# The next expert's rows: gathered in quarters and turned by VectorE, in a decoder trunk with experts

## The reference

```python
def moe_swiglu(h, router, w_gate, w_up, w_down):
    t = h.reshape(B * S, D)                                   # 256 x 1024
    top_vals, top_idx = lax.top_k((t @ router), TOP_K)        # TOP_K = 2
    gates = jax.nn.softmax(top_vals, axis=-1)
    combine = jnp.sum(jax.nn.one_hot(top_idx, N_EXPERTS) * gates[..., None], axis=1)
    out = jnp.zeros_like(t)
    for e in range(N_EXPERTS):                                # 8; w_gate[e], w_up[e] are 1024 x 3584, w_down[e] 3584 x 1024
        out = out + combine[:, e:e + 1] * swiglu(t, w_gate[e], w_up[e], w_down[e])
    return out
```

## Time and profile before

| | us |
|---|---|
| Median of three runs (lowest, highest) | 1290.2 (1289.7, 1292.92) |
| Profiled execution | 1289.74 |
| Its span, first to last instruction | 1287.9 |
| TensorE busy | 1272.9 (99%) |
| TensorE weight loads | 745.1 (58%) |
| VectorE busy | 383.6 (30%) |
| ScalarE busy | 246.4 (19%) |
| GpSimd busy | 62.5 (5%) |
| DMA, mean rate over the span | 333 GB/s |
| TensorE's granted clock, mean | 0.998 |

### The profile page before, as it was taken

The page is one execution under the profiler, slowest core; times in us unless marked ns, Lnnn a source line. Parts: engine busy times, 40 slices in busy tenths (PEclk is TensorE's granted clock), DMA queues, the critical chain, the costliest instruction groups (busy, mean ns, idle before and its releaser), DMA issues.

```text
span 1287.9 us, 30972 instructions
## 1 busy us (share of the span) xinstructions
PE 1272.9 (99%) x14108; PEld 745.1 (58%) x14108; DVE 383.6 (30%) x664; ACT 246.4 (19%) x367; POOL 62.5 (5%) x63
## 2 busy tenths in 40 slices
PE   9999999999999999999999999999999999999997
PEld 7888888888785455336335534633543453363354
DVE  6976766568753120111002012010201201110022
ACT  6774443454631100100010010001001001000102
POOL 3000000000100001000100100010010010001000
PEclk9999999999999999999999999999999999999999
DMA  9646653755259999999999999999999999999991
GB/s 316 224 144 198 206 184 122 231 192 163 74 205 395 407 412 427 412 392 421 409 403 413 416 413 396 424 409 400 417 410 408 406 424 412 397 417 409 406 375 45
DMA packets 105690, 429.29 MB, mean 333 GB/s; under 512 B 5990, under 2 KB 42576, under 8 KB 89184
## 3 DMA queue, kind: packets, MB, share of 16 engines
q1 hardware_dynamic: 100336, 417.70, 82.3%
q0 software_dynamic: 4816, 8.59, 2.6%
q10 hardware_dynamic: 416, 1.09, 0.2%
HBM read 421.05 MB, written 6.31 MB: 332 GB/s over the span
## 4 chain that ended last, share of the span: by engine, by line
PE 95%; issue 2%; DVE 2%; ACT 1%; POOL 0%; DVEq 0%; POOLq 0%; ACTq 0%
PE bank L1716 93%; PE bank L2211 1%; PE bank L1759 0%; PE bank L1956 0%; ACT h L1015 0%; ACT work L1015 0%; POOL split_area L853 0%; DVE x L1665 0%; DVE split_area L643 0%; DVE work L1511 0%; PE bank L2165 0%; DVE split_area L1264 0%; DVE h L1365 0%; ACT work L1026 0%; DVE work L1436 0%
## 5 line engine op out<-in xcount | busy, mean ns | idle before, releaser
L1716 PE MATMUL bank<-raw_area,late_area 128*32 128x448 f32 (+1 forms) x5760 | 438.6, 464 | 0.0
L1716 PE MATMUL bank<-late_area 128*32 128x448 f32 (+1 forms) x5760 | 438.4, 464 | 0.0
L1716 PEld LDWEIGHTS bank<-raw_area,late_area 128*32 128x32 f32 x5760 | 205.6, 110 | 223.3 <-issue 177.0
L1716 PE MATMUL bank<-split_area 128*128 128x512 f32 (+1 forms) x1848 | 331.0, 339 | 1.1 <-DVE split_area L1264 0.8
L1716 PEld LDWEIGHTS bank<-late_area 128*32 128x32 f32 x5760 | 194.3, 110 | 238.1 <-issue 180.9
L1716 PEld LDWEIGHTS bank<-split_area 128*128 128x128 f32 x1848 | 283.4, 189 | 42.6 <-issue 4.1
L643 DVE TENSOR_TENSOR split_area<-raw_area,split_area 128x2048 fp32r<-128x2048 f32 (+1 forms) x56 | 123.4, 2209 | 47.0 <-ACT split_area L621 47.0
L621 ACT CAST split_area<-raw_area 128x2048 fp32r<-128x2048 f32 (+1 forms) x59 | 107.7, 1833 | 71.7 <-PE bank L1716 70.0
L1627 DVE COPY slot_sum<-next_slots 32x3 f32<-32x3 f32 x96 | 15.2, 159 | 305.6 <-DMA sum_dram<-qT,slot_row 279.1
L1646 DVE SCALAR_TENSOR_TENSOR work<-bank,slot_sum,work 128x448 f32<-128x448 f32 x48 | 32.8, 684 | 233.0 <-PE bank L1716 229.4
L1141 ACT COPY late_area<-bank 128x384 f32<-128x384 f32 x9 | 4.3, 478 | 433.9 <-PE bank L2211 433.9
(11 more groups left out here) (207 smaller groups left out, 421.5 us busy)
## 6 DMA issues: line engine op xcount, KB each, us to landing
raw_area<-in_moe_w_gate SPq DMA_DIRECT2D x32, 1792.0 KB, 14.5
late_area<-in_moe_w_gate SPq DMA_DIRECT2D x32, 1792.0 KB, 13.6
raw_area<-in_moe_w_up SPq DMA_DIRECT2D x32, 1792.0 KB, 14.6
late_area<-in_moe_w_up SPq DMA_DIRECT2D x32, 1792.0 KB, 15.2
raw_area<-in_moe_w_down SPq DMA_DIRECT2D x32, 1536.0 KB, 13.0
late_area<-in_moe_w_down SPq DMA_DIRECT2D x32, 1536.0 KB, 12.4
raw_area<-in_sb_w_qkv SPq DMA_DIRECT2D x12, 1024.0 KB, 5.3
raw_area<-in_ffn_w_down SPq DMA_DIRECT2D x11, 1024.0 KB, 4.9
```

The lines of the kernel that those rows point to most:

```text
L1716: return nc.tensor.matmul(out, lhsT, rhs, start=start, stop=stop, **kw)
```

## The change

GpSimd gathers the next expert's rows in three transfers, one for each chunk of slots. The copy of `h` in DRAM is seen as four rows of 256 features for each token, and partition `32 q + s` of a chunk gets quarter `q` of slot `s`. VectorE's transpose turns blocks of 32 x 32 in place, so that partition `32 q + f` of tile `t` holds feature `256 q + 32 t + f`. It does so behind its last block of up; TensorE's transposes, the two copies out of PSUM and their banks' uses go. Since the features now lie in another order on partitions, a gate or up load takes, for tile `t`, four blocks of 32 rows of the matrix, 256 rows apart. The first gather, on TensorE, makes the same order with four products of 32 stationary columns where it had one of 128. The spreading of slots over partitions moves to behind "next", as the gathers' row numbers come from it. TensorE waits for the turned rows at the start of an item, and the last scatter waits for the banks of up in place of those of the gather.

```diff
@@ SyncE, expert_loads
-                        src = a["moe_w_" + kind][0][bass.ds(e, 1), t * P:(t + 1) * P, :].rearrange("o d f -> (o d) f")
-                        sp.dma_start(slot, src).then_inc(arrived, 16)
+                        src = a["moe_w_" + kind][0][bass.ds(e, 1), :, :].rearrange("o (q t f) n -> t (o q) f n", q=GROUPS, t=DT)
+                        sp.dma_start(slot, src[t]).then_inc(arrived, 16)
@@ GpSimd
             def rows_for_next(i):
-                taken(pool, "next", i)
-                pool.sem_inc(pool_steps, 1)
-                pool.indirect_dma_start(out=h_rows, out_offset=None, in_=h_dram[:, :],
-                                        in_offset=bass.IndirectOffsetOnAxis(next_token[0:CAP, 0:1], 0)).then_inc(rows_gathered, 16)
+                pool.wait_ge(next_rows_ready, i * CHUNKS + CHUNKS)
+                for c in range(CHUNKS):
+                    pool.sem_inc(pool_steps, 1)
+                    pool.indirect_dma_start(out=h_rows[:, c, :], out_offset=None, in_=h_dram[:, :],
+                                            in_offset=bass.IndirectOffsetOnAxis(next_row[c][:, 0:1], 0)).then_inc(rows_gathered, 16)
@@ ScalarE, item
-                gathered_part("gather", i)
@@ VectorE
+            def slots_spread():
+                steps.settle()
+                for j in range(GROUPS):
+                    for c in range(CHUNKS):
+                        ins = V.tensor_copy(next_sum[j * QUAD:(j + 1) * QUAD, c, :], next_slots[c * QUAD:(c + 1) * QUAD, :])
+                link(ins)
 
             def item(i):
                 dve.wait_ge(summed, i * SUMS + SUM_STARTS)
-                for j in range(GROUPS):
-                    for c in range(CHUNKS):
-                        ins = V.tensor_copy(slot_sum[j * QUAD:(j + 1) * QUAD, c, :], next_slots[c * QUAD:(c + 1) * QUAD, :])
-                link(ins)
+                link(V.tensor_copy(slot_sum[:, :, :], next_sum[:, :, :]))
...
                 p = full(dve, "next", i)
-                steps.mark(V.tensor_copy(next_slots[0:CAP, :], p[0:CAP, 0:3]))
-                freed(V.tensor_copy(next_token[0:CAP, :], p[0:CAP, 0:1]), "next")
+                freed(V.tensor_copy(next_slots[0:CAP, :], p[0:CAP, 0:3]), "next")
+                taken(dve, "next", i)
+                slots_spread()
+                for c in range(CHUNKS):
+                    V.scalar_tensor_tensor(next_row[c][:, :], next_sum[:, c, 0:1], float(GROUPS), quarter[:, c:c + 1],
+                                           ALU.mult, ALU.add).then_inc(next_rows_ready, 1)
...
-                gathered_part("gather", i)
+                dve.wait_ge(rows_gathered, i * (16 * CHUNKS) + 16 * CHUNKS)
+                for c in range(CHUNKS):
+                    V.transpose(gathered[:, :, c * QUAD:(c + 1) * QUAD],
+                                h_rows[:, c, :].rearrange("p (t f) -> p t f", t=DT)).then_inc(gathered_ready, 1)
@@ TensorE
             def first_gather():
-                for q in range(2):
-                    pe.wait_ge(h_ready, TB + 1 + q)
-                    b = begin(pe, ("first gather", q))
-                    for n in range(4):
-                        for tb in range(TB):
-                            t = 4 * q + n
-                            ins = mm(b[:, n * CAP:(n + 1) * CAP], h[:, tb, t * P:(t + 1) * P], place[:, tb, :],
-                                     tb == 0, tb == TB - 1)
-                    filled(ins, ("first gather", q))
-            def transposed_rows(i):
-                pe.wait_ge(rows_gathered, i * 16 + 16)
-                for q in range(2):
-                    b = begin(pe, ("gather", q), i)
-                    for n in range(4):
-                        t = 4 * q + n
-                        ins = nc.tensor.transpose(b[:, n * CAP:(n + 1) * CAP], h_rows[:, t * P:(t + 1) * P], ident[0:CAP, 0:CAP])
-                    filled(ins, ("gather", q))
+                outs = [begin(pe, ("first gather", part)) for part in range(2)]
+                for tb in range(TB):
+                    pe.wait_ge(h_ready, DH * (tb + 1))
+                    for part in range(2):
+                        for n in range(HALF_T):
+                            for q in range(GROUPS):
+                                c0 = q * OUT + (part * HALF_T + n) * QUAD
+                                ins = mm(outs[part][quad(q), n * CAP:(n + 1) * CAP], h[:, tb, c0:c0 + QUAD], place[:, tb, :],
+                                         tb == 0 and n == 0, tb == TB - 1, skip_group_check=True)
+                        if tb == TB - 1:
+                            filled(ins, ("first gather", part))
...
-                    if j == 1:
-                        transposed_rows(i)
...
-            def item(i):
-                begin(pe, ("g", 1), i)
+            def item(i, first=False):
+                if first:
+                    taken(pe, ("first gather", 0))
+                else:
+                    pe.wait_ge(gathered_ready, i * CHUNKS)
```

## The result

The changed kernel takes 2983.2 us, median of six runs (2972.8 to 3000.9), beside 1290.1 us (1289.7 to 1293.1) for the kernel before on the same chip: a ratio of 2.312, interval 2.3066 to 2.3175. The profiled execution took 2993.52 us for a span of 2991.8. Predicted were 2900 us, with 2780 to 3025 as the range of its own case (A), and 2780 to 5080 with that of rival B.

The account below looks back on a forecast made before the run. TensorE's matmuls bound the kernel before; afterwards four engines' loads would. Their work from 358.6 us ends at 2857, and tail and end give 2881 us at full clock or 2927 at the lower; taken 2900, range 2780 to 5080.

Parts of the forecast that it names:

- case (A): Gate and up loads: four engines, each at its present rate; 2780 to 3025 us, chance 0.50.
- rival B: Gate and up loads: four engines, pairs sharing one way into memory, 34.3 us a load; 3025 to 5080 us, chance 0.32.
- Four engines for a load: Gate and up loads: outermost dimension 4 leaves 4 engines where 16 served; 12 fewer small packets a load.
- 17.15 us a load: Gate and up loads: each of four engines moves 458,752 B at 26.75 GB/s, 17.15 us instead of 4.3.
- The sum: Four engines' work from 358.6 us: 2178 gate and up, 287 down, 33.5 software queue; last down landed at 2857 us.
- The tail: TensorE's work behind the last down landing: 9.9 us at full clock, 55.7 at 1.2 GHz.
- dropped transposes: TensorE's chain in each item: 0.81 us x 8 = 6.5 us off, lost if four engines serve the loads.
- The lag of the loads: Gate and up loads on sixteen engines: issue to landing grows to 23 us at the end, under 31.9, so not binding.
- rival C: Gate and up loads: all sixteen engines share them by rows, transposes' gain stays; 1282.8 us, chance 0.13.
- Rival D: Loads on sixteen engines, but scattered memory places or small gather packets cost the queue; 1287 to 1292 us, chance 0.05.

Follow-up runs that it names:

- old line: Changed kernel with each gate or up load again one block of 128 matrix rows, everything else of the change kept: 1285.23 us, ratio 0.9956.
- every-eighth kernel: Changed kernel with features ordered 8 p + t, so a load takes every eighth matrix row, 128 at one pitch: 1285.55 us, ratio 0.9958.

## Why the prediction was right, point by point

**Four engines for a load: right.** Small packets fall from 5990 to 4710, by 1280: twelve for each of 128 loads is 1536, less 256 small ones that three gathers in place of one add to the software queue (5072 packets for the 4816 of the earlier trace rows). On the queue of the loads itself the count is exact: 100336 packets before, 98800 after, 1536 fewer. The mean busy share of sixteen engines is 0.395, within the 0.3 to 0.5 named. Two and eight blocks follow the same cut. The Trainium skill, "DMA: Bandwidth & Descriptors", section "Why a DMA increments its semaphore by 16 and not by 1", had the rule, and the traces agree in all these counts.

**17.15 us a load: right**, 17.1 measured, and 34.2 and 8.55 beside it.

**Engines in each other's way, rival B: it happens, but not for long.** The trace of after shows the first gate load alone and the time behind it:

```profile
338.00:342.00 4.00, 3.78 (x24) 3.05 (x23) 2.42 (x4) 3.65 (x5) 0.83 (x1) 1.00 0.26 61
...
354.00:358.00 4.00, 4.00 (x22) 3.48 (x22) 3.34 (x4) 2.45 (x4) 0.39 (x1) 1.00 0.27 79
...
374.00:378.00 4.00, 4.00 (x20) 3.30 (x19) 1.39 (x1) 0.36 (x1) 0.00 (x0) 1.00 0.25 104
```

Four engines are busy throughout, yet they move 61 GB/s, then 79, then 104, and the first load is through after some 28 us (the rates of 334 to 362 us add up to its 1.8 MB); the 19 us of A and the 36 of B were both off. As the text put it, an engine that runs some rows ahead frees both; the rates with four and, later on, with eight blocks fit that. A loss that looks the same comes back behind down, for some 40 us in the item shown and for less in others. The runs with sixteen blocks and with four transfers show what it costs where it lasts: half the rate. The Trainium skill, "SBUF — State Buffer", section "Door 1: The DMA port swizzle", puts partitions 32 apart on one port and those 64 apart on different ones. All five readings agree with that: engines that begin 32 partitions apart (four, eight, sixteen blocks) start at half of 27 GB/s each, sixteen on 32 partitions move 228 GB/s, and two that begin 64 apart have 27 each from the start. Which engine writes which partitions is in no trace, so the pairs themselves are inferred from these rates.

**The sum: 104 us short at the last down load, and 10 us long behind it.** It had the last down landed at 2857 us; it was about 2961. From there the forecast of 2900 had 43 us, and the profiled execution has 32.5. Two terms were mis-sized.
- The start. The sixth up load should be in at 358.6 + 13 x 17.15 = 581.6 us and is taken up at 604.3. That is 23 us, the slow first loads and the other transfers up to 400 us, which the sum had at nothing; some of it is the software queue's, which the sum had apart.
- Around down. The sum gave an item 16 x 17.15 + 35.9 + 33.5/8 = 314.5 us. The pair of last up loads comes at 647.25 us in the first item and 2932.16 in the last, 326.4 us apart, so 12 us an item were missed. The sum took the four engines at their full rate beside and behind down's burst, from a row in which all loads were alike; the run with down on four engines shows that this was the error. The parts by the trace: 8.4 us at the last pair, 1.3 at the up load before it, 5.6 behind down (2.2 of them the scatters'), 1.7 beside the gathers, less the 4.2 that the sum had for the software queue. They add up to 12.8, near the 12.

**The tail.** Behind the last pair the text had 9.9 us beyond down's landing at the full clock and 55.7 at the lower one, and sat between. The windows show 0.80 for the first ten us and 1.00 from then on:

```profile
2932.00:2942.00 10.00, 9.84 (x88) 3.41 (x92) 5.41 (x9) 0.00 (x0) 0.00 (x0) 0.80 0.88 299
2942.00:2960.00 18.00, 18.00 (x332) 11.04 (x328) 4.64 (x12) 0.00 (x0) 0.00 (x0) 1.00 1.02 401
```

The last two up loads and down take 47.4 us (45.8 at the full clock), and the last down load lands some 29 us into them, not 35.9. So the tail is 18 us. With down's halves at 18.32 us in every item, the clock costs 1.6 us here: where it is at 0.7, TensorE waits for loads anyway. The lower level was a misplaced worry, and it happened to cover the two terms above: 2900 was nearer than its parts deserved.

**Other terms.** The items' gain from the dropped transposes was put at 6.5 us and is 5.8 (old line) to 7.5 (every eighth). VectorE's transposes take 402 ns (369 by columns). A gather takes GpSimd 985 ns (947 to 1560), three of them 3.0 us. The first gather takes 2.85 us (2.6 to 3.2 by the bounds); but 1.15 and 1.05 us of idle time follow it, and the first gate product starts at 400.60 against 399.44, so +1.2 us where -0.4 was taken and +0.5 was the bound. What was left out is time between instructions. The lag of the loads, which rival C put at 23 us by the last expert, is 20.5 us in the every-eighth kernel; C's 1282.8 us, for the kernel that does what the change was meant to do, stands against 1285.55. The start accounts for most of that: it is 2.8 us later where 0.4 earlier was taken, less the 1.0 us that the items gained beyond 6.5. Rival D fell with it: with the old line of loads the items are shorter by 5.8 us, so the gathers cost the queue nothing that shows, and in the every-eighth kernel rows that don't lie together cost nothing either. The gathers' packets didn't shrink to 1 KB, as the text had them: from 1150 to 1235 us the software queue has 144 packets for three gathers, 48 of them small, and 0.39 MB in the other 96, which is 4 KB each.

## What to carry to other kernels

Before the order of rows of a load is changed, read what its pattern's outermost dimension becomes: 128 rows at one pitch, every row or every eighth, kept all sixteen engines (1285.2 and 1285.6 us), while four blocks of 32 cost a factor of 2.3, in one line that leaves the bytes as they were. If an order in blocks is wanted by a 32 x 32 transpose, put the stride inside the transpose's input, where an idle engine pays for it. And a DMA share of 0.25 or 0.5 that doesn't move was engines left out in these runs; a share of 1.0 at half the usual rate fits engines that share a way.

## What the runs showed of the hardware

- Busy share isn't rate: sixteen engines at a share of 1.0 moved 428 GB/s in the kernel before, 229 with sixteen blocks, 228 with transfers of 32 rows, and 217 with down beside loads of four blocks.
- Half the rate passed off with four blocks (61 to 104 GB/s within 40 us) and with eight (115 at first, 216 at 812 us), and not with sixteen (229 GB/s at 740 us). Why it stays there wasn't tried.
- A transfer on four engines is slowed by ones on sixteen beside it: 8.4 us on two up loads. Behind those the four alone are slow for a while, 83 GB/s for 20 us in the item shown.
- SyncE's issue itself stood for up to 36 us in the changed kernel, here for a down load; those for down in the kernel before take 0.3 to 3.7 us:

```profile
891.85 35.93 SPq L786 DMA_DIRECT2D raw_area<-in_moe_w_down  x1
```

- Stationary columns that lie eight apart load in 334 ns for 128 (192 as neighbours) and 140 ns for 32 (110); a transpose of 128 x 256 values on VectorE takes 608 ns with such an input and 402 without.
- Behind the 128 narrow matmuls of the first gather TensorE stood with nothing in the profile to wait for, in every kernel that ran them at the full clock, but not equally long: about 1.0 us with two blocks and with down in four, 2.2 in the changed kernel, 2.7 with the old line of loads, 5.4 with four transfers and 5.6 with sixteen blocks. It is no fixed price of the matmuls, then. The trace has a candidate that wasn't tried: a packet of the queue of instructions (q8) moves 2 to 3 us before TensorE goes on, at 398.0 to 398.5 us for 400.62 with the old line, at 401.0 to 401.5 for 403.83 with sixteen blocks, and with two blocks, where the wait is short, at 395.0 to 395.5, ahead of the gather. Where all sixteen engines are taken at half the rate the packet comes latest.
- The clock's fall to 0.50 between 394 and 400 us in the every-eighth kernel stays open too; at most 2.8 us of that kernel's time hang on both.
